# Loading the first activations from ScalarE's queue instead of SyncE's in a one-core hybrid decoder step

## The reference

```
p = x @ w_in                                  # 1024 -> 512 (a) + 512 (u) + 512 (v)
a = p[:, :512];  u, v = split(gelu(p[:, 512:]))
a_out = pooled(a, windows 2/4/8/16) @ pool_w * pool_scale
vn    = group_norm(v)                          # 4 head groups
b_out = u * (W_s @ vn + b)                     # inside chunks of 128 positions
x = LN(alpha*x + concat(a_out, b_out) @ w_out)
x = LN(alpha*x + MoE(x))                       # 16 experts, best group of 4, then top 2
```

## Time and profile before

| | |
|---|---|
| median of three runs | 1334.17 us |
| the profiled execution's own time | 1334.49 us |
| its span, first to last instruction | 1332.7 us |
| mean granted TensorE clock | 0.911 of full speed |
| PE busy | 1110.5 us, 83% of the span |
| DVE / ACT / POOL busy | 524.7 / 294.3 / 145.6 us |
| chain that ended last: PE / DVE / issue / DMA | 76% / 9% / 7% / 4% |
| q1 (SyncE) / q0 (GpSimd) / q10 (ScalarE) | 148.43 / 77.66 / 16.78 MB |

### The profile page before, as it was taken

One profiled execution on the slowest core, in us unless ns is written; L12 is line 12 of the kernel. 1 busy time (PEld: TensorE's weight loads), 2 busy tenths in 40 slices (PEclk: granted clock), 3 DMA queues, 4 the chain that ended last, 5 costly groups with the idle time before them and its releaser, 6 DMA issues.

```text
span 1332.7 us, 18666 instructions
## 1 busy us (share of the span) xinstructions
PE 1110.5 (83%) x7162; PEld 676.4 (51%) x7162; DVE 524.7 (39%) x1342; ACT 294.3 (22%) x681; POOL 145.6 (11%) x177
## 2 busy tenths in 40 slices
PE   7999991999994399999999989876599749999910
PEld 3685541544442257776888866543345324444400
DVE  2561354111110735596455555643223631111145
ACT  0101121211111223232343313433211211111111
POOL 0010003000001100000211115122100120000030
PEclk9999995999997599999999978987799869999965
DMA  9466028999964322033333106033510589999351
GB/s 359 185 270 91 0 86 325 365 373 367 369 228 179 105 108 83 32 123 118 104 106 106 62 1 249 17 127 147 195 60 1 210 320 359 366 359 373 142 189 63
DMA packets 62754, 244.17 MB, mean 183 GB/s; under 512 B 7840, under 2 KB 28384, under 8 KB 45120
## 3 DMA queue, kind: packets, MB, share of 16 engines
q1 hardware_dynamic: 41056, 148.43, 31.1%
q0 software_dynamic: 16992, 77.66, 16.1%
q10 hardware_dynamic: 4608, 16.78, 3.2%
HBM read 203.55 MB, written 56.06 MB: 195 GB/s over the span
## 4 chain that ended last, share of the span: by engine, by line
PE 76%; DVE 9%; issue 7%; DMA 4%; ACT 2%; POOL 1%; POOLq 0%; DVEq 0%; SPq 0%; ACTq 0%
PE bank L1207 17%; PE bank L1148 10%; PE bank L1227 8%; PE bank L1353 8%; PE bank L1277 5%; PE bank L1450 4%; PE bank L1295 3%; PE bank L1197 2%; DVE acc L2247 2%; DVE stat L2045 1%; PE bank L1327 1%; PE bank L1704 1%; PE bank L1136 1%; DVE x L2062 1%; DVE x L2063 1%
## 5 line engine op out<-in xcount | busy, mean ns | idle before, releaser
L1148 PE MATMUL bank<-ring,cat 128*128 128x512 f32 (+1 forms) x320 | 142.2, 600 | 1.9 <-ACT cat L1833 1.3
L1207 PE MATMUL bank<-ring,work 128*128 128x512 f32 x256 | 113.5, 595 | 0.0
L1353 PE MATMUL bank<-xT,ring 128*128 128x288 f32 x448 | 110.9, 407 | 0.0
L2227 DVE TENSOR_TENSOR work<-work,bank 128x256 f32<-128x256 f32 x32 | 13.5, 422 | 218.6 <-ACT work L1812 218.6
L1353 PEld LDWEIGHTS bank<-xT,ring 128*128 128x128 f32 x448 | 84.6, 190 | 24.1 <-issue 1.5
L1148 PEld LDWEIGHTS bank<-ring,cat 128*128 128x128 f32 (+1 forms) x320 | 56.8, 182 | 75.3 <-issue 74.6
L1207 PEld LDWEIGHTS bank<-ring,work 128*128 128x128 f32 x256 | 48.0, 193 | 53.9 <-issue 53.9
L1197 PE MATMUL bank<-const,work 128*128 128x128 f32 x256 | 36.6, 292 | 32.5 <-DMA work<-xrows 32.5
L1277 PE MATMUL bank<-xT,ring 128*128 128x288 f32 x256 | 63.1, 407 | 0.0
L1136 PE MATMUL bank<-const,x 128*128 128x128 f32 (+1 forms) x120 | 18.5, 309 | 49.3 <-DVE x L2063 49.3
L1227 PE MATMUL bank<-ring,work 128*128 128x512 f32 x128 | 57.7, 593 | 1.0 <-issue 1.0
(11 more groups left out here) (429 smaller groups left out, 1932.6 us busy)
## 6 DMA issues: line engine op xcount, KB each, us to landing
ring<-in_stream_dram SPq DMA_DIRECT2D x71, 1024.0 KB, 8.1
cat<-in_stream_dram SPq DMA_DIRECT2D x16, 1024.0 KB, 9.0
work<-xrows ACTq DMA_DIRECT2D x32, 512.0 KB, 5.2
xT<-in_stream_dram SPq DMA_DIRECT2D x16, 1024.0 KB, 8.5
work<-in_stream_dram SPq DMA_DIRECT2D x16, 1024.0 KB, 10.2
yrows<-work POOLq DMA_DIRECT2D x32, 512.0 KB, 9.2
by_batch<-in_pages_dram SPq DMA_DIRECT2D x128, 128.0 KB, 2.4
xrows<-work POOLq DMA_DIRECT2D x1, 8192.0 KB, 28.4
```

The lines of the kernel that those rows point to most:

```text
L1148: i = pe.matmul(bank(n)[0:ROWS[tile], :], cat[:, k, tok(tile)], slot(w[k // 4], 4, 512)[:, k % 4, :], start=(k == 0), stop=(k == KC - 1))
L1207: i = pe.matmul(bank(n), xgT[:, e % 2, k, :], sparse_slot(layer, 3 * e + k // 4, 4, 512)[:, k % 4, :], start=(k == 0), stop=(k == KC - 1))
L1353: i = pe.matmul(bank(n + s)[:, 0:nn], slot(w, KC, 256)[:, k, P * (m % 2):P * (m % 2) + P], xT[:, k, a:a + nn], start=(k == 0), stop=(k == ...
```

## The change

All five loads of `xT` move from SyncE's queue to ScalarE's, where they are the first five instructions. SyncE then issues ring blocks 0 to 3 first, `const` behind block 3 instead of behind block 2, and `x_t` behind block 4 as before. GpSimd no longer waits for `xT` before it issues `even`.

```diff
@@ block.sync
-            def load_xT(tile):
-                sp.dma_start(xT[:, :, tok(tile)], A["xT"][:, KC * P * tile:KC * P * tile + KC * ROWS[tile]]
-                             .rearrange("p (c t) -> p c t", c=KC)).then_inc(xT_loaded[tile], 16)
-
-            load_xT(0)
             n = 0
             while n < len(BLOCKS):
                 key = BLOCKS[n][0]
-                if n == 2:
-                    for tile in range(1, NT):
-                        load_xT(tile)
-                if n == 3:
+                if n == 4:
                     sp.dma_start(const[:, :], A["const"]).then_inc(const_loaded, 16)
                 if n == 5:
                     sp.dma_start(x_t[:, :], A["x"]).then_inc(x_loaded, 16)
@@ block.gpsimd
-            pool.wait_ge(xT_loaded[NT - 1], 16)
             pool.dma_start(even, A["even"]).then_inc(even_loaded, 16)
             pool.wait_ge(cleared, 1)
@@ block.scalar
             step = stepper(act, act_step)
+            for tile in range(NT):
+                act.dma_start(xT[:, :, tok(tile)], A["xT"][:, KC * P * tile:KC * P * tile + KC * ROWS[tile]]
+                              .rearrange("p (c t) -> p c t", c=KC)).then_inc(xT_loaded[tile], 16)
```

## The result

The changed kernel took 1357.59 us (median of 4 runs, 1356.73 to 1358.41) against 1333.93 us for the kernel before (4 runs): a ratio of 1.0177, 95% interval [1.016, 1.0196]. It is slower by 23.7 us. The forecast was 1340.5; the direction was right and the size was not. The profiled execution took 1357.87 us with a span of 1356.1, against 1332.7 before, so the spans differ by 23.4 us.

The account below looks back on a forecast made before the run. The prediction took TensorE's start, waiting for `xT` tile 0 and ring block 0, to bound the kernel. Service of 10.6 us against 4.3 added 6.3 to the median 1334.2, giving 1340.5 us; range 1334.5 to 1363.

Parts of the forecast that it names:

- What bounds the stretch: First 120 us: TensorE's chain sets the end, busy 108.76 of 109.30 us, so its start time decides.
- the rigid shift: Everything behind TensorE's start was taken to move by the same amount, with v still about 37 us long.
- One packet per queue and turn: DMA engines at the start: one packet from each queue in turn, whatever its size, so 512-byte `xT` packets wait for 8 KB ones.
- I take the first end: Start: SyncE's issues held up behind ScalarE's blocked `xT` tile 1; service 10.6 us against 4.3, +6.3 us, chance 0.40.
- The 0.02 us of the earlier trace: At 242 us, ScalarE's issue took 0.35 us beside SyncE's against 0.33 alone; read as leaning to a shared issue path.
- the first rival: Start: SyncE not held up, `xT` tile 0 ends behind the whole first batch; +28.2 us, about 1362 us, chance 0.32 with in-between cases.
- the in-between case: Start: tile 0's starvation cut off during `x_t`, whose packets are 20 KB; about +22 us, chance counted within the 0.32.
- The forecast's own sum: Start: two ring blocks 5.0, tile 0 1.8, `even` 3.7, together 10.6 us against 4.3: +6.3 us.
- rival 2: Start: several 512-byte pieces go in one turn, tile 0 needs 8 turns; +1.4 us, 1335.6 us, chance 0.10.
- Not slower: Start: ScalarE's tile 0 is written whole before ring block 0, today's order; 0 +- 0.7 us, about 1334 us, chance 0.14.
- faster: Start: at best 0.5 us gained from the issue order, under what can be told apart; chance 0.04.

## Why the prediction was right or wrong

*What bounds the stretch, and the rigid shift: right.* TensorE ran through once started, v was 0.4 us shorter and no stretch behind it changed its length, and the start's 24.0 us less that 0.4 account for the 23.7 us of the whole.

*One packet per queue and turn: right, for 512-byte packets too*, which the trace of before could not show; 328 against 328 shows it, and the runs with 256-byte, 9 KB and joined 4 KB packets test it three ways. ScalarE's queue did start later (q10's first packets after 3.5 us), which the prediction did not have and which alone is worth under 4 turns.

*The failed step: "I take the first end", SyncE held up behind ScalarE's tile 1.* SyncE's last four DMAs went out between 2.13 and 4.35 us, beside a ScalarE issue that stood from 1.89 us on for 25.95 us. Nor was it tile 1 that stalled: ScalarE had issued tiles 0 and 1 by 1.86 us, and tile 2 was blocked. The kernel before had the same, which the merged row hid; there tile 1 took 0.43 us and tile 2 stood for 3.28:

```profile
2.81 3.28 SPq L919 DMA_DIRECT2D xT<-in_xT_dram  x1
```

The 0.02 us of the earlier trace rows that I leaned on were no sign of a blocked issue holding the other engine. The Trainium skill (Perfetto Trace Analysis, section "DMA Instruction - HWDGE (DVE, Sync)") speaks of a generator locked for one sequencer. Here a load that was waiting for room in ScalarE's queue did not lock it against SyncE. With that, the case was the first rival, to which I gave 0.32 and which the range reached.

*The size of that rival: 28.2 us predicted, 24.0 measured.* I let tile 0 outlast all of SyncE's first batch, 56 packets per engine. It landed at 31.74 us, and by 31 us q1 had moved 8.53 of its 9.74 MB:

```profile
q1 hardware_dynamic: 933, 8.53, 68.2%
q0 software_dynamic: 352, 2.87, 22.2%
q10 hardware_dynamic: 1064, 0.54, 5.9%
```

The missing 1.2 MB at 0.41 MB per us are 2.9 of the 4.2 us (counted at 31.7 us, with 8.84 MB moved, 2.2); the rest I did not take apart. Tile 0 was cut free during `x_t`, as the in-between case said (+22), for two reasons that the counts show. Each DMA's completion is a packet of its own and takes a turn as well: up to 34 us, before `x_t` is complete, q1 has moved 992 packets, 62 per engine, which is seven loads of 8 and six completions, and the 328 against 328 of 20 to 28 us hold 45 such packets under 512 bytes. And when q1 went from ring block 0 to block 1, at 5.0 to 5.8 us, it paused, and q10 moved 226 packets, 14 per engine, at one stroke:

```profile
q10 hardware_dynamic: 226, 0.12, 48.7%
q1 hardware_dynamic: 32, 0.13, 39.8%
q0 software_dynamic: 5, 0.06, 18.0%
```

The cause of the pause stays open. In the same 0.8 us q10 moves 224 packets where GpSimd's loads come late, 223 where SyncE is held, and 465 where tile 0 is in 256-byte pieces. Where `xT` comes from GpSimd's queue there is no pause: q1 keeps the engines busy for 97.8% of 4 to 6 us. So something of ScalarE's many small pieces may still touch SyncE's queue, for less than a microsecond; no run shows what.

*The forecast's own sum would have been short as well.* Made by hand, its case costs 9.1 us at the start instead of 6.3. The missing term is GpSimd's `bufT` and LN parameters, about 3.1 us by the estimate above, which I had left out although I counted them in the first rival.

*Turns balanced by bytes (rival 2)* fell for ScalarE's queue. The Trainium skill (DMA: Bandwidth & Descriptors, section "Queues, rings and completion order") gives 9 to 17 descriptors to a packet, typically. Here pieces are joined only in GpSimd's queue, eight to a packet of 4 KB, and from ScalarE's every 512-byte piece was a packet and a turn (SyncE's 512-byte pieces too are counted one by one). *Not slower* and *faster* fell with the start at 31.8 us.

## What to carry to other kernels

A load in small pieces should not share the DMA engines with loads in large ones while somebody waits for it: in every run here it got turns, not bytes. Count the packets per engine of the load that is waited for, and multiply by the time of one packet of each queue that stands beside it; here 64 turns beside 0.315 us (8 KB), 0.466 us (12.3 KB) and 0.77 us (20 KB, from 28 to 32 us: 0.998 x 64 / 83). Such a count is an estimate: it gave 28.2 us where 24.0 were measured. Keep such a load ahead of the large ones in the same queue, or make its pieces large. The second issuing engine saved nothing here but issue time: ring block 0 was issued at 0.75 us instead of 1.25, and the start came 24.0 us later. Where TensorE waits at the start, cutting the first loads so that the first product needs fewer bytes gained 2.5 us, about what the bytes take.

## What the runs showed of the hardware

A ScalarE DMA issue that waits for room (25.95 us) does not hold up SyncE's issues (0.44 to 0.72 us each beside it). DMA engines take one packet per queue and turn, down to packets of 512 and 256 bytes (328 against 328 in 8 us, with 3.28 MB against 0.17 and 3.31 against 0.08). Completion packets count as turns (992 packets in q1 for 896 of data). The same access pattern travels as 512-byte packets from SyncE's and ScalarE's queues and as 4 KB packets from GpSimd's. TensorE, idle for 10.4 us, restarts at a granted clock of 0.50.
